# Reading the spill count during the last scatter, and splitting two tiles of the final norm between GpSimd and ScalarE

## Chip, cores and metric

The kernel runs on one core of a Trainium2 chip. The metric is device time in microseconds (us), the median of several executions. The five engines are TensorE (PE in the profile), VectorE (DVE), ScalarE (ACT), GpSimd (POOL) and SyncE (SP, which only issues DMAs here). The core has 16 DMA engines.

## What is computed

One layer of a decoder on 1024 prompt tokens and 64 sample tokens of width 1024: a mixing block, cross attention, a mixture of 32 SwiGLU experts (each token goes to 2), and a last RMSNorm. The change touches the end of the mixture and the last norm:

```python
def rmsnorm(x, g):
    xf = x.astype(jnp.float32)
    y = xf * lax.rsqrt(jnp.mean(xf * xf, axis=-1, keepdims=True) + EPS)
    return (y * g.astype(jnp.float32)).astype(x.dtype)
...
x = x + hier_moe(rmsnorm(x, g_ffn), w_rg, b_rg, w_re, b_re, w_e1, w_e3, w_e2)
...
y_prompt = rmsnorm(xp, g_final)
y_sample = rmsnorm(xs, g_final)
```

## The kernel before

The 1088 tokens lie in nine tiles of 128 rows (tile 8, the sample tokens, has 64), in X, a view of the SBUF region regX. The program of each engine is written out by hand, and semaphores order them.

**Experts.** The sums so far are stored to `token_sums` in HBM. Then for each of 32 experts GpSimd gathers up to 128 token rows by an indirect DMA (`rows_in`), TensorE computes with weights that SyncE streams into a ring (which lies over regX, so X is gone by then), and GpSimd adds the weighted result to `token_sums` by an indirect DMA that accumulates (`rows_out`, L2471).

**Spills.** An expert with over 128 tokens leaves a rest, which a loop of up to 16 steps would handle. VectorE works out the number of such steps between experts 16 and 26 (`spill_counts` to `spill_columns`) and leaves it in `spx[0:1, 16:17]`. Each engine loads this number into a register after `o_go` and skips the loop where it is 0, as with these inputs. In the kernel before it is GpSimd that gives `o_go`, after the waits for the last scatters (`m_sc`), and it loads its own copy after that (L2515); then it signals `s_moe`.

**Final norm.** SyncE waits for `s_moe` and reads the nine tiles of `token_sums` back into X (L989, a helper's line; `sums_back(eng, t)` waits for tile t). ScalarE squares and sums each tile in turn (L1611) and takes a root for each group of tiles (L1614); the groups are `NORMS = [(0, 2), (2, 3), (5, 3), (8, 1)]`, first tile and count. VectorE's `finish(g)` turns the roots of a group into factors by five short steps (L2382, L1632 to L1635) and then multiplies each tile by its factor and by the gain `gfin` (a view of regA) in place (L2386), each product signalling `s_fo`. SyncE stores tile t when `s_fo` is at t + 1 (L1199), in the order 0 to 8. The gain is loaded once TensorE has used the last weights.

Of the kernel before, what the change touches and what calls it, by code (L numbers as in the profile page):

```python
# [33 lines left out]
ALU = mybir.AluOpType  # L34
# [48 lines left out]
def trunk_step(nc, i_, o_):  # L83
    ctx = ExitStack()
    with ctx:
# [3 lines left out]
        def sem(name):  # L89
            return ctx.enter_context(nc.semaphore(name))  # L90
# [205 lines left out]
        junk = regS[:, 4 * D:5 * D]  # L296
        gfin = regA[:, 7168:8192]
        NORMS = [(0, 2), (2, 3), (5, 3), (8, 1)]

        table = nc.dram_tensor("place_table", [P * NPLACE, 2], I32, kind="Internal").ap()  # L300
        xn_dram = nc.dram_tensor("normed_tokens", [N, D], F32, kind="Internal").ap()
# [119 lines left out]
        s_gos = sem("s_gos")  # L421
        s_gate = sem("s_gate")
        s_gtd = sem("s_gtd")
        s_last = sem("s_last")
        m_w = [sem(f"m_w{s}") for s in range(RAW // 2)]
        m_g = [sem("m_g0"), sem("m_g1")]
        m_sc = [sem("m_sc0"), sem("m_sc1")]
# [559 lines left out]
        def _(sp):  # L987
# [204 lines left out]
            sp.wait_ge(s_moe, 1)  # L1192
            for t in range(NT):
                load(X[0:rows_of(t), t], sum_dram[P * t:P * t + rows_of(t), :], m_w[t])
            for t in range(NT):
                sp.wait_ge(s_fo, t + 1)
                dst = o_["y_prompt"][0, P * t:P * t + P, :] if t < NPT else \
                    o_["y_sample"].rearrange("b s d -> (b s) d")
                sp.dma_start(dst, X[0:rows_of(t), t]).then_inc(s_fst, 16)  # L1199
            sp.wait_ge(s_fst, 16 * NT)  # L1200


# [1 line left out]
        def _(act):  # L1204
# [291 lines left out]
            for t in range(NT):  # L1496
                r = rows_of(t)
                emptied(act, ("O2", t, 1))
                if t >= 2:
                    act.wait_ge(s_xnd[t % 2], 16 * (t // 2))  # L1500
                if t < NT - 1:
                    norm_act(3, t, X[:, t, :])
                else:
                    c = 120 + t
                    nc.scalar.activation(junk8[0:r, :], X[0:r, t, :], ACT.Square,
                                         accum_out=stat[0:r, c:c + 1]).then_inc(s_sq[3], 1)
                if t >= 3:
                    filled(act, ("R", t - 3))
                ps, sg = filled(act, ("T", 3, t, 1))
                copy(YT3[t % 3][:, 4:8, 0:r], ps[:, :].rearrange("p (k n) -> p k n", k=4)[:, :, 0:r], sg)  # L1510
                if t == NT - 1:
                    act.wait_ge(s_sq[3], NT)
                    nc.scalar.activation(stat[0:r, c + 10:c + 11], stat[0:r, c:c + 1], ACT.Sqrt,
                                         scale=1.0 / D, bias=small[0:r, 0:1]).then_inc(s_rt[3], 1)
                    act.wait_ge(s_last, 1)
                    nc.scalar.activation(xn2[0:r, t % 2], xn2[0:r, t % 2], ACT.Copy,
                                         scale=stat[0:r, c + 20:c + 21]).then_inc(s_xn[3], 1)

# [86 lines left out]
            for t0, n in NORMS:  # L1605
                for t in range(t0, t0 + n):
                    r = rows_of(t)
                    sums_back(act, t)
                    if t > 0:
                        act.wait_ge(s_fsq, t)  # L1610
                    nc.scalar.activation(junk[0:r, :], X[0:r, t, :], ACT.Square,  # L1611
                                         accum_out=stat[0:r, t:t + 1]).then_inc(s_fsq, 1)
                act.wait_ge(s_fsq, t0 + n)
                nc.scalar.activation(stat[0:r, 10 + t0:10 + t0 + n], stat[0:r, t0:t0 + n], ACT.Sqrt,  # L1614
                                     scale=1.0 / D, bias=small[0:r, 0:1]).then_inc(s_frt, 1)


        @block.vector
        def _(dve):
# [570 lines left out]
                    place(t // GT - 1)  # L2190
            add_bias(NT - 2)
            rstd(3, NT - 1)
            nc.vector.sem_inc(s_last, 1)
            add_bias(NT - 1)
            route(2)
            place(2)
# [139 lines left out]
            for e in range(NE):  # L2336
# [25 lines left out]
                    spill_before()  # L2362
                if e == 26:
                    spill_columns()
            dve.wait_ge(o_go, 1)
            n_spill = dve.value_load(spx[0:1, 16:17], min_val=0, max_val=SPILL)
            with dve.If(n_spill > 0):
                with dve.Fori(0, SPILL) as q:
# [8 lines left out]
            def finish(g):  # L2377
                t0, n = NORMS[g]
                r = rows_of(t0)
                dve.wait_ge(s_frt, g + 1)  # L2380
                a, root, r0, tmp, out = (stat[0:r, c + t0:c + t0 + n] for c in (280, 10, 300, 310, 20))
                link(ts_(a, stat[0:r, t0:t0 + n], 1.0 / D, EPS, ALU.mult, ALU.add))  # L2382
                inv_root(a, root, r0, tmp, out)
                for j in range(n):
                    x = X[0:r, t0 + j, :]
                    stt(x, x, out[:, j:j + 1], gfin[0:r, :], ALU.mult, ALU.mult).then_inc(s_fo, 1)  # L2386

            dve.wait_ge(s_cst, 32)
            for g in range(len(NORMS)):
# [4 lines left out]
        def _(g):  # L2394
# [104 lines left out]
            for e in range(NE):  # L2499
# [4 lines left out]
                if 12 <= e < 12 + NT:  # L2504
                    g.wait_ge(s_plc, (e - 12) // GT + 1)
                    for c in range(2):
                        place_rows(e - 12, c)
            rows_out(NE - 1)
            for s in range(2):
                g.wait_ge(m_sc[s], 16 * (NE // 2))  # L2510
            g.wait_ge(s_scat, 16 * 2 * NT)
            g.wait_ge(s_gtd, 16)

            g.sem_inc(o_go, 1)
            n_spill = g.value_load(spx[0:1, 16:17], min_val=0, max_val=SPILL)  # L2515
            with g.If(n_spill > 0):  # L2516
                with g.Fori(0, SPILL) as q:
                    g.wait_ge(o_ix, 16 * q + 16)
# [6 lines left out]
                    scatter(0, oix, o_sc)  # L2525
                g.wait_ge(o_sc, 16 * (SPILL + 1))
            g.sem_inc(s_moe, 1)  # L2527
            g.wait_ge(s_outs, 16 * 6)
            g.wait_ge(s_kout, 32)

# [97 lines left out]
```

## Time and profile before

| | us |
|---|---|
| median of 3 executions (1067.07 to 1067.89) | 1067.43 |
| the profiled execution | 1065.81 |
| its span | 1064.0 |
| PE / DVE / ACT / POOL busy | 999.0 / 638.3 / 541.6 / 197.6 |
| bytes moved by the DMA engines | 203.06 MB |

Times in the rows further down are us from the start of the span. An engine with a q (POOLq, SPq) is its sequencer, which issues DMAs, loads registers and branches. A line number is that of kernel.py. "Landing" is the time at which a DMA's completion is signalled, counted from its issue. A row with x3 holds three instructions that follow each other.

### The profile page before, as it was taken

How to read it: one execution, taken by the hardware profiler on the slowest of the kernel's cores; microseconds unless marked ns; L12 is line 12 of the kernel's file. 1: busy time of each engine (PE TensorE's matmuls, PEld its weight loads, DVE VectorE, ACT ScalarE, POOL GpSimd, SP SyncE). 2: the span in 40 equal slices, each digit the busy share in tenths (PEclk: the TensorE clock that was granted, in tenths of full speed). 3: DMA queues.
4: the chain of work that ended last, by engine and by line, in shares of the span. 5: the costliest groups of instructions: out<-in, count | busy, mean ns of one | idle time of the engine just before them, and what ended most of it. 6: DMA issues, size and time to landing. Idle time of an engine off the chain costs nothing. (4 is left out here: it accounts for less than half of the span.)

```text
span 1064.0 us, 14237 instructions
## 1 busy us (share of the span) xinstructions
PE 999.0 (94%) x5327; PEld 848.1 (80%) x5327; DVE 638.3 (60%) x1175; ACT 541.6 (51%) x918; POOL 197.6 (19%) x136
## 2 busy tenths in 40 slices
PE   8999999999999999999999999948999999999970
PEld 6998999798887689999655878847888888888850
DVE  4526756345654650002664125677999999999935
ACT  6644333305221532213545012255999999999944
POOL 0003211100000021200000300011333375642220
PEclk9999999999999999999999999967999999999995
DMA  9701111244000653103563005487999999999738
GB/s 314 217 1 59 57 42 40 99 139 173 1 1 0 225 177 113 40 20 127 232 256 139 1 37 201 159 310 300 396 392 391 384 364 390 382 387 393 284 55 335
DMA packets 55211, 203.06 MB, mean 191 GB/s; under 512 B 10710, under 2 KB 19423, under 8 KB 41575
## 3 DMA queue, kind: packets, MB, share of 16 engines
q1 hardware_dynamic: 44327, 181.61, 44.9%
q0 software_dynamic: 10816, 20.54, 7.6%
q8 instruction: 43, 0.70, 0.3%
q14 instruction: 25, 0.20, 0.1%
HBM read 185.06 MB, written 32.83 MB: 205 GB/s over the span
## 5 line engine op out<-in xcount | busy, mean ns | idle before, releaser
L527 PE MATMUL bank<-regA_r,regW_r 128*128 128x352 f32 (+1 forms) x456 | 148.8, 326 | 0.0
L526 PE MATMUL bank<-regA_r,regW_r 128*128 128x352 f32 (+1 forms) x456 | 148.7, 326 | 0.0
L359 POOL TENSOR_TENSOR regW_r<-regW,regW_r 128x1024 fp32r<-128x1024 f32 x19 | 47.1, 2477 | 348.7 <-ACT regW_r L346 348.6
L1525 ACT ACTIVATE regY_r<-expert_w 128x1024 fp32r<-128x1024 f32 x105 | 108.9, 1062 | 1.0 <-PE bank L527 0.9
L525 PE MATMUL bank<-expert_w_r,regS_r 128*128 128x512 f32 x256 | 103.4, 404 | 0.0
L1525 ACT ACTIVATE regW_r<-expert_w 128x1024 fp32r<-128x1024 f32 x87 | 90.2, 1061 | 6.7 <-PE bank L527 6.7
L2292 DVE TENSOR_TENSOR expert_w_r<-expert_w,regY_r 128x1024 fp32r<-128x1024 f32 x74 | 89.0, 1218 | 0.0
L525 PE MATMUL bank<-regY_r,regW_r 128*128 128x352 f32 (+1 forms) x264 | 87.3, 331 | 0.5 <-ACT regB L1206 0.5
L526 PEld LDWEIGHTS bank<-regA_r,regW_r 128*128 128x128 f32 x456 | 85.9, 188 | 0.4
L527 PEld LDWEIGHTS bank<-regA_r,regW_r 128*128 128x128 f32 x456 | 85.6, 188 | 0.0
L2466 POOL DMA_INDIRECT regW<-normed_tokens,idx x32 | 44.0, 1374 | 200.0 <-DVE idx L2201 119.6
L1215 ACT ACTIVATE regS<-regX 128x1024 f32<-128x1024 f32 (+1 forms) x17 | 18.0, 1060 | 119.9 <-DVE regX L1877 119.9
L527 PE MATMUL bank<-regW_r,regA_r 128*128 128x384 f32 (+3 forms) x216 | 76.4, 354 | 0.0
L2471 POOL DMA_INDIRECT token_sums<-regS,idx x32 | 55.5, 1735 | 106.2 <-ACT regS L1548 102.6
L1877 DVE TENSOR_TENSOR regX<-regX,bank 128x512 f32<-128x512 f32 (+1 forms) x36 | 24.1, 686 | 77.8 <-PE bank L527 77.7
L527 PE MATMUL bank<-regY_r,regS_r 128*128 128x512 f32 x180 | 70.4, 391 | 0.0
L526 PE MATMUL bank<-regY_r,regB_r 128*128 128x512 f32 (+1 forms) x176 | 68.6, 390 | 0.0
L1952 DVE TENSOR_REDUCE stat<-bank 128x2 f32<-128x512 f32 x16 | 11.0, 690 | 93.9 <-PE bank L699 93.9
L2292 DVE TENSOR_TENSOR expert_w_r<-expert_w,regW_r 128x1024 fp32r<-128x1024 f32 x54 | 64.8, 1217 | 0.0
L527 PE MATMUL bank<-regY_r,regA_r 128*128 128x512 f32 (+1 forms) x164 | 64.0, 390 | 0.0
L525 PE MATMUL bank<-regB_r,regW_r 128*128 128x352 f32 (+1 forms) x192 | 63.0, 328 | 0.0
L526 PE MATMUL bank<-regY_r,regS_r 128*128 128x512 f32 x148 | 57.7, 390 | 0.0
(363 smaller groups left out, 2408.1 us busy)
## 6 DMA issues: line engine op xcount, KB each, us to landing
expert_w<-in_we SPq DMA_DIRECT2D x96, 1024.0 KB, 13.3
regY<-in_cache_mem_v SPq DMA_DIRECT2D x6, 1024.0 KB, 7.2
regW<-in_wbc SPq DMA_DIRECT2D x11, 512.0 KB, 3.6
regS<-in_x_prompt SPq DMA_DIRECT2D x8, 512.0 KB, 6.5
regX<-in_x_prompt SPq DMA_DIRECT2D x8, 512.0 KB, 6.6
regW<-in_wq SPq DMA_DIRECT2D x8, 512.0 KB, 3.6
regA<-in_kct SPq DMA_DIRECT2D x4, 1024.0 KB, 7.9
token_sums<-regX SPq DMA_DIRECT2D x8, 512.0 KB, 2.9
```

The lines of the kernel that those rows point to most:

```text
L359: eng.tensor_tensor(lo, raw, hi.bitcast(F32), ALU.subtract).then_inc(w_lo[name], 1)
L525: nc.tensor.matmul(out, stays[0], moves[1], start=first, stop=False)
L526: nc.tensor.matmul(out, stays[1], moves[0], start=False, stop=False)
L527: ins = nc.tensor.matmul(out, stays[0], moves[0], start=False, stop=last)
L1215: nc.scalar.activation(dst[0:r, :], src[0:r], ACT.Square, accum_out=stat[0:r, c:c + 1]).then_inc(s_sq[s], 1)
L1525: nc.scalar.activation(part_hi[u % HI], part_raw[n % RAW], ACT.Copy).then_inc(m_wh, 1)
L1877: tt(x, x, ps[0:r, :], ALU.add).then_inc(sg, 1)
L1952: link(nc.vector.tensor_reduce(stat[:, 276:278], ps[:, :].rearrange("p (a m) -> p a m", a=2), axis=AX.X, op=ALU.max, negate=True))
L2292: tt(part_lo[n % RAW], part_raw[n % RAW], part_hi[u % HI].bitcast(F32), ALU.subtract).then_inc(m_ul, 1)
L2466: g.indirect_dma_start(out=XG[s], out_offset=None, in_=xn_dram, in_offset=bass.IndirectOffsetOnAxis(ap=ix[:, 0:1], axis=0), bounds_check=l ...
L2471: g.indirect_dma_start(out=sum_dram, out_offset=bass.IndirectOffsetOnAxis(ap=ix[:, 0:1], axis=0), in_=YO[s], in_offset=None, bounds_check= ...
```

## The change

It has two parts. The spill count: VectorE gives `o_go` itself, behind the last step of the count (expert 26), and GpSimd loads the count before it waits for the last scatters. The final norm: for tiles 6 and 7 GpSimd multiplies X by the gain into another place (`WEIGHTED`, in regY, where weights lay), and ScalarE scales that by the tile's factor, once tile 5's product on VectorE has signalled. VectorE leaves these two tiles out. SyncE keeps its order of stores and takes tiles 6 and 7 from the new place. `s_last`, which ordered a step much earlier, is renamed and shared with GpSimd's products.

```diff
+        POOL_ROWS = (6, 7)
+        WEIGHTED = [regY[:, 3072 + D * j:4096 + D * j] for j in range(len(POOL_ROWS))]
...
-            for t in range(NT):
-                sp.wait_ge(s_fo, t + 1)
+            by_dve, by_pool = [t for t in range(NT) if t not in POOL_ROWS], list(POOL_ROWS)
+            for t in (0, 1, 2, 3, 4, 5, 6, 7, 8):
+                if t in by_pool:
+                    sp.wait_ge(s_fo_act, by_pool.index(t) + 1)
+                else:
+                    sp.wait_ge(s_fo, by_dve.index(t) + 1)
...
-                sp.dma_start(dst, X[0:rows_of(t), t]).then_inc(s_fst, 16)
+                sp.dma_start(dst, WEIGHTED[by_pool.index(t)] if t in by_pool else X[0:rows_of(t), t]).then_inc(s_fst, 16)
...
+            for j, t in enumerate(POOL_ROWS):
+                act.wait_ge(s_rooted_weighted, 1 + j + 1)
+                act.wait_ge(s_fo, NORMS[2][0] + 1)
+                nc.scalar.activation(WEIGHTED[j], WEIGHTED[j], ACT.Copy, scale=stat[:, 20 + t:21 + t]).then_inc(s_fo_act, 1)
...
                 if e == 26:
                     spill_columns()
-            dve.wait_ge(o_go, 1)
+                    nc.vector.sem_inc(o_go, 1)
             n_spill = dve.value_load(spx[0:1, 16:17], min_val=0, max_val=SPILL)
...
-                for j in range(n):
-                    x = X[0:r, t0 + j, :]
-                    stt(x, x, out[:, j:j + 1], gfin[0:r, :], ALU.mult, ALU.mult).then_inc(s_fo, 1)
+                for t in range(t0, t0 + n):
+                    if t not in POOL_ROWS:
+                        x = X[0:r, t, :]
+                        stt(x, x, stat[0:r, 20 + t:21 + t], gfin[0:r, :], ALU.mult, ALU.mult).then_inc(s_fo, 1)
...
             rows_out(NE - 1)
+            g.wait_ge(s_scat, 16 * 2 * NT)
+            g.wait_ge(s_gtd, 16)
+            g.wait_ge(o_go, 1)
+            n_spill = g.value_load(spx[0:1, 16:17], min_val=0, max_val=SPILL)
             for s in range(2):
                 g.wait_ge(m_sc[s], 16 * (NE // 2))
-            g.wait_ge(s_scat, 16 * 2 * NT)
-            g.wait_ge(s_gtd, 16)
-
-            g.sem_inc(o_go, 1)
-            n_spill = g.value_load(spx[0:1, 16:17], min_val=0, max_val=SPILL)
...
             g.sem_inc(s_moe, 1)
+            g.wait_ge(s_cst, 32)
+            for j, t in enumerate(POOL_ROWS):
+                sums_back(g, t)
+                g.tensor_tensor(WEIGHTED[j], X[:, t, :], gfin[:, :], ALU.mult).then_inc(s_rooted_weighted, 1)
```

GpSimd's instructions after the scatters (rows of a scatter, the load of the count, the branch around the loop), in the kernel before:

```order
L2471 DMA token_sums<-regS,idx 1088x1024 [waits m_yo1,m_yo0] x6
L2515 TENSOR_LOAD spx [waits s_gtd,s_scat,m_sc0,m_sc1]
L2515 ISA x2
L2516 COMPARE_AND_BRANCH
L2517 UNCONDITIONAL_BRANCH
L2517 ISA
```

and in the changed one:

```order
L2483 DMA token_sums<-regS,idx 1088x1024 [waits m_yo1,m_yo0] x6
L2524 TENSOR_LOAD spx [waits o_go,s_gtd,s_scat]
L2524 ISA x2
L2527 COMPARE_AND_BRANCH [waits m_sc1,m_sc0]
L2528 UNCONDITIONAL_BRANCH
L2528 ISA
```

The load no longer waits for the last scatters (`m_sc0`, `m_sc1`), and the branch does.

The end of GpSimd's program, before (the end of the spill loop, and the end of the block):

```order
L2523 ISA
L2471 DMA token_sums<-regS,oix 1088x1024 [waits o_yo,s_waited]
L2517 REGISTER_ALU
L2517 COMPARE_AND_BRANCH
L2516 UNCONDITIONAL_BRANCH [waits o_sc]
L85 UNCONDITIONAL_BRANCH [waits s_kout,s_outs]
```

and now:

```order
L2534 ISA
L2483 DMA token_sums<-regS,oix 1088x1024 [waits o_yo,s_waited]
L2528 REGISTER_ALU
L2528 COMPARE_AND_BRANCH
L2527 UNCONDITIONAL_BRANCH [waits o_sc]
L2542 TENSOR_TENSOR regY<-regX,regA 128x1024 [waits m_w6,s_cst]
L2542 TENSOR_TENSOR regY<-regX,regA 128x1024 [waits m_w7]
L85 UNCONDITIONAL_BRANCH [waits s_kout,s_outs]
```

Two products of 128x1024 stand behind the signal of the sums, each waiting for its tile's read (`m_w6`, `m_w7`).

VectorE's last two groups of the norm, tiles 5 to 7 and tile 8, before:

```order
L1632 RECIPROCAL stat<-stat 128x3 [waits s_dv]
L1633 SCALAR_TENSOR_TENSOR stat<-stat 128x3 [waits s_dv]
L1634 TENSOR_TENSOR stat<-stat 128x3 [waits s_dv]
L1635 SCALAR_TENSOR_TENSOR stat<-stat 128x3 [waits s_dv]
L2386 SCALAR_TENSOR_TENSOR regX<-regX,stat,regA 128x1024 [waits s_dv]
L2386 SCALAR_TENSOR_TENSOR regX<-regX,stat,regA 128x1024 x2
L2382 TENSOR_SCALAR stat<-stat 64x1 [waits s_frt]
L1632 RECIPROCAL stat<-stat 64x1 [waits s_dv]
L1633 SCALAR_TENSOR_TENSOR stat<-stat 64x1 [waits s_dv]
L1634 TENSOR_TENSOR stat<-stat 64x1 [waits s_dv]
L1635 SCALAR_TENSOR_TENSOR stat<-stat 64x1 [waits s_dv]
L2386 SCALAR_TENSOR_TENSOR regX<-regX,stat,regA 64x1024 [waits s_dv]
```

and now:

```order
L1643 RECIPROCAL stat<-stat 128x3 [waits s_dv]
L1644 SCALAR_TENSOR_TENSOR stat<-stat 128x3 [waits s_dv]
L1645 TENSOR_TENSOR stat<-stat 128x3 [waits s_dv]
L1646 SCALAR_TENSOR_TENSOR stat<-stat 128x3 [waits s_dv]
L2398 SCALAR_TENSOR_TENSOR regX<-regX,stat,regA 128x1024 [waits s_dv]
L2393 TENSOR_SCALAR stat<-stat 64x1 [waits s_frt]
L1643 RECIPROCAL stat<-stat 64x1 [waits s_dv]
L1644 SCALAR_TENSOR_TENSOR stat<-stat 64x1 [waits s_dv]
L1645 TENSOR_TENSOR stat<-stat 64x1 [waits s_dv]
L1646 SCALAR_TENSOR_TENSOR stat<-stat 64x1 [waits s_dv]
L2398 SCALAR_TENSOR_TENSOR regX<-regX,stat,regA 64x1024 [waits s_dv]
```

Of the products of 128x1024 in the third group one is left, tile 5's, and the steps for tile 8 follow it directly.

## Rows read from the trace of the kernel before

**Rows 1.** Busy us by stretch and engine, granted clock, DMA share, GB/s.
```profile
1037.50:1039.50 2.00, 0.00 (x0) 0.00 (x0) 0.00 (x0) 0.75 (x1) 0.00 (x0) 0.50 0.00 0
...
1052.50:1062.00 9.50, 0.00 (x0) 0.00 (x0) 7.87 (x16) 2.35 (x6) 0.00 (x0) 0.50 1.03 420
```

**Rows 2.** The chain that ended last: start us, us, what.
```profile
1037.88 0.51 POOLq L2515
...
1038.70 0.06 POOLq L2516
...
1038.93 0.34 SPq L989
...
1040.73 7.05 DMA regX<-token_sums
```

**Rows 3.** Timeline of DVE, final norm: start us, us, engine line op, count.
```profile
1050.33 3.68 DVE L2386 SCALAR_TENSOR_TENSOR regX<-regX,stat,regA 128x1024 f32<-128x1024 f32 x3
...
1054.92 3.68 DVE L2386 SCALAR_TENSOR_TENSOR regX<-regX,stat,regA 128x1024 f32<-128x1024 f32 x3
...
1059.44 1.28 DVE L2386 SCALAR_TENSOR_TENSOR regX<-regX,stat,regA 64x1024 f32<-64x1024 f32 x1
```

**Rows 4.** SyncE, stores of tiles 5, 7, 8, each with us to landing.
```profile
1056.23 0.33 SPq L1199 DMA_DIRECT2D out_y_prompt<-regX  x1
...
out_y_prompt<-regX SPq DMA_DIRECT2D x1, 512.0 KB, 4.1
...
1058.63 0.33 SPq L1199 DMA_DIRECT2D out_y_prompt<-regX  x1
...
out_y_prompt<-regX SPq DMA_DIRECT2D x1, 512.0 KB, 4.2
...
1060.74 0.49 SPq L1199 DMA_DIRECT2D out_y_sample<-regX  x1
...
out_y_sample<-regX SPq DMA_DIRECT2D x1, 256.0 KB, 2.9
```

**Rows 5.** DMA issues from 540 to 740 us: KB each, median us to landing.
```profile
token_sums<-regX SPq DMA_DIRECT2D x8, 512.0 KB, 2.9
```

**Rows 6.** Instructions of line 359: ns min/median/max, first and last start.
```profile
L359 POOL TENSOR_TENSOR regW_r<-regW,regW_r x19: 2360/2410/3249, 57.2 to 461.5; 128x1024 fp32r<-128x1024 f32 x19
```

**Rows 7.** Timeline of ACT, squares of tiles 6 and 7.
```profile
1050.42 1.06 ACT L1611 ACTIVATE regS<-regX 128x1024 f32<-128x1024 f32 x1
...
1052.07 1.06 ACT L1611 ACTIVATE regS<-regX 128x1024 f32<-128x1024 f32 x1 [0.50 <-DMA regX<-token_sums]
```

**Rows 8.** POOL and DVE where they overlap; two lines' ns min/median/max.
```profile
129.37 2.40 POOL L359 TENSOR_TENSOR regW_r<-regW,regW_r 128x1024 fp32r<-128x1024 f32 x1 [14.86 <-ACT regW_r L346]
...
130.57 2.28 DVE L1746 TENSOR_TENSOR regS<-regS,regW 128x1024 f32<-128x1024 f32 x1 [5.96 <-ACT regS L1314]
...
L1746 DVE TENSOR_TENSOR regS<-regS,regW x6: 1224/1225/2279, 130.6 to 218.8; 128x1024 f32<-128x1024 f32 x6
...
159.43 2.80 POOL L359 TENSOR_TENSOR regW_r<-regW,regW_r 128x1024 fp32r<-128x1024 f32 x1 [9.61 <-ACT regW_r L346]
...
159.88 2.49 DVE L1822 TENSOR_TENSOR regS<-regS 128x128 f32<-128x128 f32 x1
...
L1822 DVE TENSOR_TENSOR regS<-regS x6: 222/329/2492, 119.4 to 163.6; 128x176 f32<-128x176 f32 x2, 64x160 f32<-64x160 f32 x1, 128x160 f32<-128x160 f32 x1, 128x128 f32<-128x128 f32 x1
...
373.36 5.84 POOL L359 TENSOR_TENSOR regW_r<-regW,regW_r 128x1024 fp32r<-128x1024 f32 x2 [120.21 <-ACT regW_r L346]
...
374.95 1.98 DVE L1894 TENSOR_TENSOR regY_r<-regY,regY_r 128x1024 fp32r<-128x1024 f32 x1 [1.37 <-ACT regY_r L1390]
```

**Rows 9.** Timeline of ACT, three conversions in a row.
```profile
1002.83 3.03 ACT L1525 ACTIVATE regW_r<-expert_w 128x1024 fp32r<-128x1024 f32 x3
```

**Rows 10.** SyncE's waits: us in total, times, longest.
```profile
SPq L989 <- POOLq L2527: 0.2, 1, 0.2
```

More of the change, by code:

```diff
@@ L423, in trunk_step @@
         s_gtd = sem("s_gtd")
-        s_last = sem("s_last")
+        s_fo_act = sem("s_fo_act")
+        s_rooted_weighted = sem("s_rooted_weighted")
         m_w = [sem(f"m_w{s}") for s in range(RAW // 2)]
@@ L1514, in _ @@
                                          scale=1.0 / D, bias=small[0:r, 0:1]).then_inc(s_rt[3], 1)
-                    act.wait_ge(s_last, 1)
+                    act.wait_ge(s_rooted_weighted, 1)
                     nc.scalar.activation(xn2[0:r, t % 2], xn2[0:r, t % 2], ACT.Copy,
@@ L2192, in _ @@
             rstd(3, NT - 1)
-            nc.vector.sem_inc(s_last, 1)
+            nc.vector.sem_inc(s_rooted_weighted, 1)
             add_bias(NT - 1)
```

## The prediction

> **What bounds the kernel now.** The change touches only the end of the program, so I read the end. The stretches come first [rows 1]: from 1052.5 to 1062 us the 16 DMA engines are full (share 1.03) and move 420 GB/s, with DVE busy for 7.87 us of 9.5 beside them; from 1037.5 to 1039.5 us nothing moves at all. The chain that ended last [rows 2] fills this gap: the last scatter lands at 1037.88, GpSimd loads the spill count (0.51 us for the load alone), branches at 1038.70, and only then does SyncE issue the first read of the sums, at 1038.93. The fifth of these reads takes 7.05 us, since it queues behind four others.
>
> Then the final norm. DVE's timeline [rows 3] shows products in packs: three in 3.68 us, of 1.28 us each, so one begins each 1.20 us. Tile 5's is the first of the pack at 1054.92 and ends at 1056.20; tiles 6 and 7 follow, then four short steps, then tile 8, which ends at 1060.72. Each product is stored as it ends [rows 4]: tile 5 issued at 1056.23 and landed 4.1 us later (1060.33), tile 7 at 1058.63 with 4.2 us (1062.83), tile 8 at 1060.74 with 2.9 us (1063.64). A store of 512 KB with a quiet queue takes 2.9 us too [rows 5]. So the 4.1 and 4.2 us are queueing: the landings of tiles 5 and 7 lie 2.50 us apart, 1.25 each, and tile 8 with half the bytes comes 0.8 us after tile 7. **The end is held by two things at once**: DVE hands over a tile each 1.20 us, and the DMA engines write one each 1.25 us. Taking work from DVE alone could give only the last 0.2 us or so (1062.83 + 0.63 for half a tile, against 1063.64).
>
> **The change, part by part.**
>
> 1. The count is read while the scatter flies. GpSimd's steps from 1037.88 to 1038.70 leave the path [rows 2]: -0.82 us. SyncE, ScalarE, VectorE and TensorE read theirs earlier too, as DVE now signals at expert 26; SyncE's issue of the reads waits for nothing else. ScalarE's table load (1.28 us) comes earlier as well, beside the scatter: no gain, since ScalarE waits for the first read anyway. Bounds: 0 (something else holds SyncE) to -1.05 (all of the gap between landing and issue). I take -0.82.
>
> 2. DVE loses the products of tiles 6 and 7: 2 x 1.20 = -2.40 us before tile 8's product, nothing before tile 5's.
>
> 3. GpSimd gains two products of 128x1024 with both inputs in SBUF. No row has this pair, but the same form of subtraction took 2.41 us in the median on GpSimd [rows 6]. Tile 6 lands by 1050.42 and tile 7 at 1052.07, where ScalarE begins on them [rows 7]; 0.82 earlier that is 1049.6 and 1051.2, in the middle of DVE's products of tiles 2 to 4. So the question is what the two engines do to each other.
>
> The places where both run answer it [rows 8]. At 129.37 GpSimd starts its subtraction (ends 131.77); DVE starts a TENSOR_TENSOR with two SBUF inputs at 130.57 and ends at 132.85, 2.28 us where this line's median is 1.225: it did nothing until GpSimd was through and then took 1.08. A whole block thus costs 2.40 - (1.225 - 1.08) = 2.25 us. At 159.88 a DVE op of 128x128 took 2.49 where its line's median is 0.33, a block of 2.16; GpSimd's, issued at 159.43 under a running DVE op, took 2.80, so it had waited too. At 374.95 (1.98) and in the 5.84 of two GpSimd ops they take turns. All of these pairs read only SBUF on both engines. The product of the norm reads X and the gain, both in SBUF. I take 2.2 us for each, 4.4 together; bounds 0 (they overlap freely) and 2.4 each.
>
> Those rows are TENSOR_TENSOR, and the norm's product is SCALAR_TENSOR_TENSOR, which no row shows beside GpSimd. Here the Trainium skill, "SBUF — State Buffer", section "Who interferes with whom", says that any DVE instruction with two SBUF inputs and a GpSimd instruction that reads SBUF exclude each other for a whole instruction. By it the sum would be the one below. Without the page, the case that only TENSOR_TENSOR collides stays open; its sum is that of the first rival.
>
> DVE is late as a consequence: tile 5's product ends at 1056.20 - 0.82 + 4.4 = 1059.8. GpSimd takes turns and is through by some 1056.6, so it is never the one waited for. Tile 8's product ends at 1060.72 - 0.82 - 2.4 + 4.4 = 1061.9.
>
> 4. ScalarE gains two scalings, and they wait for tile 5's product (s_fo at 6), though all that they need of DVE is ready before it. Nothing is queued behind them on ScalarE, but SyncE stores in the order 0 to 8, so tile 8 waits behind both. An ACTIVATE of 128x1024 takes 1.06 [rows 7] and three in a row 3.03 [rows 9], so the two end 1.1 and 2.1 us after tile 5's: tile 6 is issued at 1060.9, tile 7 at 1061.9, tile 8 0.4 later (0.33 us of issue), at 1062.3, against 1060.74 before. All 6 other stores go as before.
>
> 5. Landing. The queue was idle before tile 5 by now: 1059.8 + 2.9 = 1062.7. Tile 6 lands at 1062.7 + 1.25 = 1063.95 (its own 1060.9 + 2.9 is 1063.8), tile 7 at 1065.2, tile 8 at 1065.2 + 0.8 = 1066.0. Before: 1063.64. **Sum +2.3 us.** The bounds: if the four stores don't queue, tile 8 lands at 1062.3 + 2.9 = 1065.2, +1.6; blocks of 2.4 give +2.7; blocks of 2.0 give +1.9.
>
> The Trainium skill, "DMA: Bandwidth & Descriptors", section "Where 436 GB/s comes from", has about 358 GB/s as the HBM side's limit per core. The trace has 420 GB/s in just this stretch, so the measurement decides; by the page a tile would cost 1.46 us instead of 1.25, and the end would come some 0.5 us later still.
>
> The profiled execution took 1065.81 us (span 1064.0), 1.6 less than the median of 1067.43; the change adds the same to both, so 1067.43 + 2.3 = **1069.7 us**. A measurement of this kernel can tell about 0.2%, 2.1 us, from no change, so the forecast lies just beyond that line.
>
> **Rivals.**
> - **No collision.** If the product of the norm isn't held up by GpSimd, DVE ends tile 5 at 1055.4, ScalarE has tile 7 by 1057.5, and the DMA engines are the only bound: landings at 1.25 each from a start 0.82 earlier, tile 8 at 1062.83 - 0.82 + 0.63 = 1062.6, -1.0 us: 1066.4. It is not slower at all. It decides as soon as the two blocks together cost under 1.2 us or so: tile 5 would land at 1055.4 + 2.9 = 1058.3 by itself, and the queue gets to it at 1060.33 - 0.82 = 1059.5 only. For it: no row has this DVE form beside GpSimd. Against it: every pair with two SBUF inputs in [rows 8] collided. 0.10.
> - **Half of it.** One of the two products falls where DVE is idle or in its short steps and costs nothing. Then tile 5 is issued at 1057.6 and lands at 1060.5, and tiles 6 to 8 follow at 1061.75, 1063.0 and 1063.8: +0.1, 1067.5. For it: before the pack of tile 2 and between the packs DVE has four or five short steps and a wait. Against it: tile 6 lands (1050.4) just after that pack begins (1050.33), and a short step with two SBUF inputs is blocked as well. 0.12.
> - **The early count brings nothing**, because the chain of GpSimd after the scatter hides another wait of the same length (SyncE waits only 0.2 us for GpSimd in the table of waits [rows 10], and the landing of the scatter itself isn't in a row of its own). Then part 1 is 0: +3.1, 1070.5. 0.08.
> - **GpSimd late**: its first product in a long time is slow, or it has to let several DVE ops pass, so that tile 6 or 7 isn't there when tile 5's product ends. From 3 us later than I put it this decides; with 4 us it gives 1071. Against it: its two ops at 373 came after 120 us of idling and took 5.84 together, turns with DVE included [rows 8]. 0.04.
>
> **Numbers.** The forecast has 0.66, within 1068.8 to 1070.4 (bounds of blocks, of the queue, and 0.3 us of spread between runs). Of it a bit over half lies beyond 2.1 us, 0.36, and 0.30 within. Slower: 0.36 + 0.08 + 0.04 = 0.48. Within 0.2%: 0.30 + 0.12 + 0.08 = 0.50. Faster by over 2.1 us: 0.02, since even without any collision the DMA engines allow 1.0. The range leaves out the first rival and the top of the last: 1067.2 to 1070.9.
>
> **What would show it.** In the changed profile: the first read of the sums is issued about 0.25 us after the last scatter's landing, not 1.05. Two DVE products of the tiles 2 to 4 take some 3.4 us instead of 1.28, each beside a GpSimd product of 2.4 to 3.6 us. ScalarE's two scalings begin at tile 5's product's end. The stores of tiles 5 to 8 land 3 us after issue, and the DMA share drops below 0.8 between 1054 and 1060, where it was 1.03. Wrong would be: DVE products all at 1.28 (the first rival), a first read that comes no earlier (the third), or a ScalarE that waits for GpSimd (the fourth).

## The result

The changed kernel takes 1070.8 us (median of 20 executions, 1067.32 to 1072.79), the kernel before 1068.34 us (20 executions, 1065.69 to 1070.47). The medians lie 2.5 us apart. The ratio formed from all executions is 1.0019 with a 95% interval from 1.0011 to 1.0026: slower by 2.0 us (1.2 to 2.8). The interval does not include 1, but the size is just about what the prediction took for the least that can be told (2.1 us). The profiled execution took 1071.62 us.

Its span is 1069.8 us against 1064.0, which is more than the change did. GpSimd's first scatter starts at 751.74 us here and at 748.53 in the kernel before, and its 29th at 1015.02 and 1011.81: the 263.28 us between them are the same to the hundredth, and the 3.21 us of offset were there before the experts began; their cause is open. So I count from a mark next to the change, the issue of the last scatter. From there to the end of the span it is 1064.0 - 1033.82 = 30.18 us before and 1069.8 - 1037.05 = 32.75 us now: **+2.57 us**.

**The start of the tail.** The chain that ended last in the changed kernel, start us, us, what:

```profile
1037.05 4.12 DMA token_sums<-regS,idx
...
1041.26 0.06 POOLq L2527
...
1041.48 0.34 SPq L992
...
1043.29 7.14 DMA regX<-token_sums
```

The last scatter is issued at 1037.05 and lands 4.12 us later (before: 1033.82 to 1037.88, 4.06). Then comes the branch, and the first read of the sums is issued at 1041.48, 0.31 us after the landing, where [rows 2] had 1.05: 0.74 us gained. The fifth read takes 7.14 us, as before.

**The collision.** Timelines of DVE and POOL in the changed kernel, final norm:

```profile
1052.96 1.28 DVE L2398 SCALAR_TENSOR_TENSOR regX<-regX,stat,regA 128x1024 f32<-128x1024 f32 x1
...
1054.17 3.36 DVE L2398 SCALAR_TENSOR_TENSOR regX<-regX,stat,regA 128x1024 f32<-128x1024 f32 x1
...
1057.45 3.37 DVE L2398 SCALAR_TENSOR_TENSOR regX<-regX,stat,regA 128x1024 f32<-128x1024 f32 x1
...
1053.07 3.38 POOL L2542 TENSOR_TENSOR regY<-regX,regA 128x1024 f32<-128x1024 f32 x1 [14.47 <-DMA regX<-token_sums]
...
1056.43 3.31 POOL L2542 TENSOR_TENSOR regY<-regX,regA 128x1024 f32<-128x1024 f32 x1
...
1052.96 7.85 DVE L2398 SCALAR_TENSOR_TENSOR regX<-regX,stat,regA 128x1024 f32<-128x1024 f32 x3
...
1061.73 1.28 DVE L2398 SCALAR_TENSOR_TENSOR regX<-regX,stat,regA 128x1024 f32<-128x1024 f32 x1
...
1063.85 1.28 DVE L2398 SCALAR_TENSOR_TENSOR regX<-regX,stat,regA 64x1024 f32<-64x1024 f32 x1
```

The first two rows and the third are tiles 2, 3 and 4. Tile 2's product began 0.11 us before GpSimd's and took its usual 1.28; GpSimd's took 3.38, since it first waited for that one. Tile 3's took 3.36, tile 4's 3.37: each stood until GpSimd was through. The pack of three takes 7.85 us where [rows 3] had 3.68, 4.17 more for two products of GpSimd, 2.09 each. Tile 5's product ends at 1063.01, 4.26 us later after the first read's issue than before (21.53 against 17.27).

**The scalings and the stores.** ACT's two scalings, and SyncE's last stores, each with its time to landing:

```profile
1063.11 2.19 ACT L1626 ACTIVATE regY<-regY,stat 128x1024 f32<-128x1024 f32 x2 [3.89 <-DVE regX L2398]
...
1063.05 0.33 SPq L1206 DMA_DIRECT2D out_y_prompt<-regX  x1
...
out_y_prompt<-regX SPq DMA_DIRECT2D x1, 512.0 KB, 2.6
...
1064.29 0.33 SPq L1206 DMA_DIRECT2D out_y_prompt<-regY  x1
...
out_y_prompt<-regY SPq DMA_DIRECT2D x1, 512.0 KB, 2.7
...
1065.70 0.49 SPq L1206 DMA_DIRECT2D out_y_sample<-regX  x1
...
out_y_sample<-regX SPq DMA_DIRECT2D x1, 256.0 KB, 3.7
```

ScalarE begins when tile 5's product is there. Tile 5's store has nothing ahead of it and lands after 2.6 us, where [rows 4] had 4.1; tiles 6 and 7 take 2.7 and 3.0 us, each landing 1.3 us behind the tile before. Tile 8's takes 3.7, since it is issued 0.4 us after tile 7's. Tile 8 lands at 1069.4.

**The DMA engines** by stretch (the columns of [rows 1]: DMA share and GB/s last):

```profile
1057.00:1059.50 2.50, 0.00 (x0) 0.00 (x0) 2.50 (x2) 2.16 (x6) 2.50 (x1) 0.50 1.03 419
1060.00:1061.50 1.50, 0.00 (x0) 0.00 (x0) 1.40 (x5) 0.00 (x0) 0.00 (x0) 0.50 0.16 63
1063.00:1064.00 1.00, 0.00 (x0) 0.00 (x0) 0.83 (x7) 0.89 (x1) 0.00 (x0) 0.50 0.15 57
```

They were full to the end before [rows 1] and now run dry twice, at 1060 and at 1063, because DVE hands over no tile. From 1064 on they are full again to the end.

### The profile page after: what moved, and what is told of

Read it like the earlier page. It is cut to its first block, busy times and chain, and to the rows that moved or that the text cites. A ratio compares the mean times of both kernels' runs of the same rounds, so it can differ in the third digit from the quotient of the medians.

```text
span 1069.8 us, 14242 instructions
## 1 busy us (share of the span) xinstructions
PE 1000.1 (93%) x5327; PEld 849.2 (79%) x5327; DVE 640.1 (60%) x1173; ACT 543.9 (51%) x920; POOL 204.5 (19%) x138
## 4 chain that ended last, share of the span: by engine, by line
PE 59%; DVE 17%; DMA 2%; ACT 2%; issue 2%; ACTq 0%; SPq 0%; POOLq 0%; DVEq 0%
PE bank L528 15%; PE bank L530 15%; PE bank L529 15%; DVE expert_w_r L2303 6%; PE bank L496 4%; DVE expert_w_r L2309 3%; PE bank L702 3%; PE bank L505 2%; PE bank L893 1%; DVE regS_r L2321 1%; DVE regX L2398 1%; PE bank L773 1%; PE bank L753 1%; DMA regW<-normed_tokens,idx 1%; DMA regX<-token_sums 1%
## 5 line engine op out<-in xcount | busy, mean ns | idle before, releaser
L1222 ACT ACTIVATE regS<-regX 128x1024 f32<-128x1024 f32 (+1 forms) x17 | 18.0, 1059 | 120.0 <-DVE regX L1888 120.0
```

## The experiments

Times of the tail come from one trace each; ratios to the kernel before with their intervals from several runs of both. "Tail" is counted from the issue of the last scatter, "from the first read" from the issue of the first read of the sums, "from the first landing" from the start of the first square on ScalarE, and "from the pack" from the start of VectorE's products of tiles 2 to 4, where the first collision comes. The first three carry the spread of the DMA engines: the scatter lands after 3.7 to 4.1 us in these traces and the first read after 3.3 to 4.0, and the pack starts between 7.6 and 8.6 us after the first square. The last leaves that out, and it repeats to 0.1 us between traces of the same norm.

| kernel | ratio (95% interval) | tail | from the first read | from the first landing | from the pack |
|---|---|---|---|---|---|
| before | 1 | 30.18 | 25.07 | 21.37 | 13.67 |
| changed | 1.0019 (1.0011 to 1.0026) | 32.75 | 28.32 | 25.00 | 16.84 |
| changed again (e12) | 1.0012 (0.9999 to 1.0025) | 32.72 | 28.75 | 24.79 | 16.79 |
| count alone (e1) | 0.9990 (0.9978 to 1.0002) | 29.22 | 25.16 | 21.30 | 13.69 |
| count alone again (e11) | 0.9993 (0.9979 to 1.0008) | 29.03 | 25.01 | 21.24 | 13.62 |
| norm alone (e2) | 1.0022 (1.0011 to 1.0033) | 33.30 | 28.21 | 24.49 | 16.87 |
| gain in PSUM (e3) | 0.9990 (0.9980 to 1.0000) | 30.11 | 26.02 | 22.41 | 13.77 |
| halves in SBUF (e4) | 1.0017 (1.0005 to 1.0028) | 32.77 | 28.68 | 24.96 | 17.35 |
| idle products (e5) | 1.0028 (1.0018 to 1.0037) | 33.72 | 29.36 | 25.43 | 17.82 |
| one tile (e6) | 1.0006 (0.9995 to 1.0017) | 30.73 | 26.39 | 22.35 | 14.75 |
| scalings early (e7) | 1.0022 (1.0011 to 1.0032) | 32.28 | 28.30 | 24.53 | 16.92 |
| gain in PSUM, scalings early (e8) | 0.9992 (0.9981 to 1.0003) | 29.71 | 25.60 | 21.61 | 14.00 |
| stores held (e9) | 1.0008 (0.9997 to 1.0020) | 31.28 | 27.08 | 23.66 | 15.95 |
| product in idle time (e10) | 0.9987 (0.9973 to 1.0002) | 31.23 | 26.93 | 23.16 | 14.80 |

My theory: the early count gives 0.75 us, and GpSimd's products stop VectorE's for 2.1 us each, since both engines read two SBUF tensors. The rivals: the two parts depend on each other; the products are slow for another reason (the stores and reads that pass through the same tiles, ScalarE's wait, the order of the stores).

### The parts apart

e1 has only the count's part (the edit against the kernel before, with `o_go` given behind `spill_columns`); e2 is the changed kernel with this edit undone:

```diff
-            dve.wait_ge(o_go, 1)
+                    nc.vector.sem_inc(o_go, 1)
...
+            g.wait_ge(o_go, 1)
+            n_spill = g.value_load(spx[0:1, 16:17], min_val=0, max_val=SPILL)
             for s in range(2):
                 g.wait_ge(m_sc[s], 16 * (NE // 2))
-            g.sem_inc(o_go, 1)
-            n_spill = g.value_load(spx[0:1, 16:17], min_val=0, max_val=SPILL)
```

> Only the early load of the count; the norm as before. The tail is counted from the issue of the last scatter to the end of the span: 30.2 us in the kernel before, 32.8 in the changed one. Theory (the two parts are independent, the count gives 0.75 us, the collision of GpSimd and VectorE takes it back and more): tail 29.4 to 29.6, landing of the scatter to first read 0.3 us, nine products of 1.28 us, total 0.7 us below the kernel before. Rival (the early count brings nothing to the end, since the DMA engines or a later wait bound it): first read earlier but tail 30.0 to 30.2.

> Only the split of tiles 6 and 7; the count as before. Theory: tail 33.4 to 33.6 (32.8 + 0.75), two products of VectorE of 3.3 to 3.4 us beside GpSimd's two of 3.3, total 2.7 to 3.3 us above the kernel before. Rival (the two parts interact, for instance the late landing of tile 7's read, 14.9 us after the first read's issue against 13.1, comes from the early count): tile 7 lands after 13.1 us here and the tail is 32 or less.

The count alone has a tail of 29.22 us, 0.96 less than before (0.74 of it between landing and first read, 0.3 a scatter that landed after 3.75 us), and from the first read on it is the kernel before (25.16 against 25.07). The norm alone takes 33.30 us, 3.12 more than before, all of it behind the first read. Both tails lie just under the ranges I gave (29.4 to 29.6, and 33.4 to 33.6). -0.96 and +3.12 give +2.16 against the +2.57 of both together; the 0.4 us left are no more than what the landings of the scatter and of the first read differ by. Without these landings the sum closes: from the pack the count alone is the kernel before (13.62 and 13.69 against 13.67), and the norm alone is the changed kernel (16.87 against 16.84 and 16.79). Tile 7's square starts 13.0 us after the first read's issue in e2, as its rival had it, but the tail is 33.30 and not 32. So the parts add up, and neither rival stands.

### Is it the second SBUF input?

ScalarE has nothing to do between the scatter and the first read. In e3 it copies the gain into two free PSUM banks there, and VectorE takes it from them in halves of 512 columns; VectorE waits for these two copies before its first product, and SyncE's count of ScalarE's signals allows for them. All the rest, GpSimd's products included, is the changed kernel, which the edit is against. e4 is the control, with the loop over halves and `gfin[0:r, 512 * h:512 * h + 512]` in place of the bank.

```diff
+            act.wait_ge(s_cst, 32)
+            for h in range(2):
+                nc.scalar.activation(bank[B_TX[h]][:, :], gfin[:, 512 * h:512 * h + 512], ACT.Copy).then_inc(s_fo_act, 1)
...
-                        x = X[0:r, t, :]
-                        stt(x, x, stat[0:r, 20 + t:21 + t], gfin[0:r, :], ALU.mult, ALU.mult).then_inc(s_fo, 1)
+                        for h in range(2):
+                            x = X[0:r, t, 512 * h:512 * h + 512]
+                            ins = stt(x, x, stat[0:r, 20 + t:21 + t], bank[B_TX[h]][0:r, :], ALU.mult, ALU.mult)
+                        ins.then_inc(s_fo, 1)
```

> The changed kernel, with the gain copied by ScalarE into two PSUM banks while it waits for the first read, and VectorE's products taking it from there in two halves of 512 columns, so that they read SBUF once. GpSimd's products and ScalarE's scalings stay. Theory (two engines that both need a second SBUF read exclude each other): no product of VectorE is stretched (two halves take 1.3 to 1.4 us), GpSimd's two take 2.4 each, tile 5's product ends 4 us earlier, and the DMA engines bound the end: tail 29.2 to 29.8. Rival (the products are slow for another reason, such as the stores and reads that move through X at the same time): the same stretches of 3.3 us, tail 32.8 or more.

> The control for the one with the gain in PSUM: the products of VectorE in the same two halves, but both inputs in SBUF. Theory: GpSimd waits for one half and not for a whole product, VectorE loses the same 2.1 us or so per product of GpSimd: tail 32.6 to 33.4. Rival (the halves themselves let the engines interleave): tail below 31.

Timelines of DVE and POOL with the gain in PSUM:

```profile
1051.93 4.04 DVE L2402 SCALAR_TENSOR_TENSOR regX<-regX,stat,bank 128x512 f32<-128x512 f32 x6
1055.88 0.85 DVE L2396 TENSOR_SCALAR stat<-stat 128x3 f32<-128x3 f32 x1
1056.77 0.17 DVE L1646 RECIPROCAL stat<-stat 128x3 f32<-128x3 f32 x1
...
1052.03 4.67 POOL L2547 TENSOR_TENSOR regY<-regX,regA 128x1024 f32<-128x1024 f32 x2 [14.89 <-DMA regX<-token_sums]
```

Beside GpSimd's two products, which take 4.67 us together, VectorE's six halves take 4.04 us, 1.35 per tile: none of them waits. The control:

```profile
1051.65 8.25 DVE L2399 SCALAR_TENSOR_TENSOR regX<-regX,stat,regA 128x512 f32<-128x512 f32 x6
...
1051.79 5.57 POOL L2544 TENSOR_TENSOR regY<-regX,regA 128x1024 f32<-128x1024 f32 x2 [14.01 <-DMA regX<-token_sums]
```

8.25 us for the same six halves (GpSimd waits for a half only, hence 5.57 for its two). The products differ in nothing but where the gain lies, and with it in PSUM the 4.2 us are gone. That settles the cause of the stretch: the product's second input in SBUF. The time follows: 0.9990 against 1.0017. The tail of e3 is 30.11 us, though, and I had put it at 29.2 to 29.8. The reads of the second group came late in this execution: the pack starts 12.25 us after the first read's issue (before: 11.40), and from the pack to the end it is 13.77 us against 13.67. Tile 5's product ends 2.2 us earlier after the first read than in the changed kernel (19.3 against 21.5), not the 4 us expected, for the same reason and because of the row that follows.

One row of e3 I had not expected: VectorE's TENSOR_SCALAR on 3 columns of `stat` took 0.85 us instead of 0.17. It reads one SBUF tensor; it began at 1055.88 and ended at 1056.73, just behind GpSimd's second product (1056.70). In e8 the same step takes 0.89 us and ends just behind GpSimd too (1056.55 against 1056.51). So that form is held up as well, [rows 8] have none of it, and "two inputs in SBUF" is not the whole rule.

### The collision by itself

e5 is the count alone with all nine products on VectorE, and GpSimd's two products beside them, whose result nobody uses. VectorE waits before tiles 6 and 7 until GpSimd has read them.

```diff
+            for j, t in enumerate(POOL_ROWS):
+                sums_back(g, t)
+                g.tensor_tensor(WEIGHTED[j], X[:, t, :], gfin[:, :], ALU.mult).then_inc(s_idle, 1)
...
+                    if t0 + j in POOL_ROWS:
+                        dve.wait_ge(s_idle, POOL_ROWS.index(t0 + j) + 1)
```

> The early count, and the norm as before with all nine products on VectorE, but GpSimd computes its two products of tiles 6 and 7 as well and nobody uses them (VectorE multiplies these two tiles only once GpSimd has read them). This measures the collision by itself. Counted from the issue of the first read of the sums to the end of the span: 25.1 us before, 25.2 with the count alone, 28.3 in the changed kernel. Theory: 2.1 us lost per product of GpSimd and nothing taken from VectorE: 25.1 + 4.2 = 29.3, two products stretched to 3.3 us. Rival (part of the loss in the changed kernel is ScalarE's scalings and the order of the stores, and a product of GpSimd alone costs VectorE less): below 28.3.

Timelines of DVE and POOL with the idle products:

```profile
1051.68 7.86 DVE L2391 SCALAR_TENSOR_TENSOR regX<-regX,stat,regA 128x1024 f32<-128x1024 f32 x3
...
1060.45 3.68 DVE L2391 SCALAR_TENSOR_TENSOR regX<-regX,stat,regA 128x1024 f32<-128x1024 f32 x3
...
1051.82 6.63 POOL L2535 TENSOR_TENSOR regY<-regX,regA 128x1024 f32<-128x1024 f32 x2 [14.49 <-DMA regX<-token_sums]
```

7.86 us again in place of 3.68, then an undisturbed pack of 3.68. From the first read it is 29.36 us, 4.2 more than the count alone; 29.3 was expected. From the pack to the end it is 17.82 us, where the changed kernel has 16.84. So taking the two products off VectorE gave back 1.0 us of the 2.4 that VectorE itself was relieved of.

e6 is the changed kernel with only tile 7 split off.

```diff
-        POOL_ROWS = (6, 7)
+        POOL_ROWS = (7,)
```

> The changed kernel with only tile 7 split off. Counted from the first read's issue: theory 25.9 to 26.2 (one block of 2.1 us, one product of 1.2 us less before tile 8's product: 25.1 + 0.9), total some 0.2 us from the kernel before. Rival (the loss comes from waiting for ScalarE after tile 5 and not from the number of blocks): near the 28.3 of two tiles.

One block: the pack of three takes 5.77 us, 2.09 more than 3.68. From the first read it is 26.39 us, a little over the range I gave (25.9 to 26.2), with a first landing 4.0 us after the issue that was late by 0.3; the rival's 28.3 is far. The stretch of the pack goes by the number of blocks. The end does not quite: from the pack it is 1.1 us later with one block (14.75 against 13.67) and 3.2 with two. An explanation that no run tests by itself: before the change tile 5's store stood in the DMA queue (4.1 us to landing against 2.6 in e6), which hides part of the first block and nothing of the second.

### Where ScalarE's wait matters

In e7 ScalarE waits for the factors of tiles 5 to 7 and not for tile 5's product; e8 does the same with the gain in PSUM. The edit, against the changed kernel:

```diff
-                act.wait_ge(s_rooted_weighted, 1 + j + 1)
-                act.wait_ge(s_fo, NORMS[2][0] + 1)
+                act.wait_ge(s_rooted_weighted, 1 + 2 + 1)
...
+                if g == 2:
+                    nc.vector.sem_inc(s_rooted_weighted, 1)
```

> The changed kernel, but ScalarE waits for the factors of tiles 5 to 7 and not for tile 5's product. Counted from the first read's issue: theory (the end hangs on ScalarE's scalings only by their start behind tile 5's product; then on VectorE's product of tile 8): the scalings begin 1.3 us earlier, tile 8 is issued at 23.7 and the end is at 26.9 to 27.3. Rival (the DMA engines hold the end already): 28.0 or more.

> The gain in PSUM for VectorE, and ScalarE waiting for the factors only. Counted from the first read's issue: with the gain in PSUM alone it was 26.0, where ScalarE's scalings ended at 21.6. Theory: now they end by 20.1, tile 8's product at 21.5, and the end is that of the DMA engines, 24.7 to 25.1; total 1.0 to 1.5 us below the kernel before. It can't go lower, since nine reads and nine stores of 1.25 us each (tile 8 less) with 3.5 us ahead of the first landing make 25. Rival (VectorE's or SyncE's issue of the stores is the bound): 24.2 or less, or still 26.

e7 was a miss. The scalings begin 20.2 us after the first read instead of 21.6, and the end stays at 28.30. SyncE's stores in e7, with their times to landing (the last row holds two, tiles 6 and 7):

```profile
1061.58 0.33 SPq L1206 DMA_DIRECT2D out_y_prompt<-regX  x1
...
out_y_prompt<-regX SPq DMA_DIRECT2D x1, 512.0 KB, 2.6
...
1061.95 1.26 SPq L1206 DMA_DIRECT2D out_y_prompt<-regY  x2
...
out_y_prompt<-regY SPq DMA_DIRECT2D x2, 512.0 KB, 4.1
```

Tile 5 is issued when its product is there and lands after 2.6 us; tiles 6 and 7 follow at once and take 4.1 us (their median), since they stand in the DMA queue. From tile 5's store on, three and a half tiles have to go through, and they take as long whether ScalarE is early or not: 6.3 us from its issue to tile 8's landing in e7, 6.35 in the changed kernel. That is the rival that I had written down for e7, that the DMA engines hold the end already. My first reading of the changed kernel's trace, that ScalarE's wait was the last link, was wrong: that wait lies beside the DMA time. What holds the end is the moment at which tile 5's store is issued, as part 5 of the prediction had it.

With the gain in PSUM (e8) the scalings end by 19.5, and it takes 21.61 us from the first landing against 21.24 to 21.37 of the count alone and the kernel before. The 25.60 from the first read miss my range of 24.7 to 25.1, mostly by what the first landing was late (4.0 us). From the pack it is 14.00 us, 0.3 more than the count alone: between 1059 and 1060 us the DMA share is 0.63, since tile 5's product comes late by the held-up TENSOR_SCALAR (0.89 instead of 0.17 us) and the slower halves (4.04 instead of 3.68 for the pack). So e8 is no faster than the count alone. But it is not the split at no cost: these two delays are its own. That the split could win nothing even without them is argued from the rates before the change, and not shown.

### Two experiments on the DMA engines

e9 has the count alone and issues no store before tile 8's read has landed. In e10, with the count alone too, GpSimd weights tile 0 in the time in which VectorE waits for the first root, and VectorE only scales it; SyncE stores tile 0 from the new place. The edit of e9, then that of e10:

```diff
+            sums_back(sp, NT - 1)
             for t in range(NT):
                 sp.wait_ge(s_fo, t + 1)
```

```diff
+            sums_back(g, 0)
+            g.tensor_tensor(WEIGHTED, X[:, 0, :], gfin[:, :], ALU.mult).then_inc(s_idle, 1)
...
+                    if t0 + j == 0:
+                        dve.wait_ge(s_idle, 1)
+                        ts_(WEIGHTED, WEIGHTED, out[:, 0:1], None, ALU.mult).then_inc(s_fo, 1)
+                        continue
```

> The count alone, and SyncE issues no store before tile 8's read has landed. In the traces so far the DMA rate falls from 420 to about 250 GB/s for 2 us or so, where the first two stores join the last reads. Counted from the start of the first square (the first landing): the end comes 21.3 us after it with the count alone. Theory (reads and stores mixed cost rate, some 0.8 us): tile 8's read lands 0.7 to 1.2 us sooner than 11.05 us after the first, but the stores start up to 1.5 us late, end 21.3 to 22.5. Rival (tile 8's read with its 64 rows is slow by itself): it lands no sooner, end 22.5 or more.

> The count alone, and one product on GpSimd, that of tile 0, which lands while VectorE still waits for the first root; VectorE then scales tile 0 by a TENSOR_SCALAR with one SBUF tensor as input, and does the other eight products as before. Theory (only overlap costs): GpSimd takes 2.4 us, no VectorE product is stretched, VectorE's scaling takes 0.6 to 0.8 us instead of 1.28; the end is still the DMA engines', 21.2 to 21.5 us after the first square's start. Rival (a product on GpSimd costs wherever it stands): some 2 us more, or a stretched operation.

In the kernel before, the rate drops while the first stores join the last reads; in e9 it stays up for longer. Stretches of half a microsecond, first of the kernel before, then of e9:

```profile
1050.50:1051.00 0.50, 0.00 (x0) 0.00 (x0) 0.50 (x1) 0.50 (x1) 0.00 (x0) 0.50 0.90 246
1051.00:1051.50 0.50, 0.00 (x0) 0.00 (x0) 0.50 (x1) 0.50 (x2) 0.00 (x0) 0.50 0.90 270
```

```profile
1051.50:1052.00 0.50, 0.00 (x0) 0.00 (x0) 0.40 (x4) 0.45 (x2) 0.00 (x0) 0.50 1.03 418
1052.00:1052.50 0.50, 0.00 (x0) 0.00 (x0) 0.50 (x1) 0.46 (x1) 0.00 (x0) 0.50 1.06 426
1052.50:1053.00 0.50, 0.00 (x0) 0.00 (x0) 0.50 (x1) 0.50 (x2) 0.00 (x0) 0.50 1.12 336
1053.00:1053.50 0.50, 0.00 (x0) 0.00 (x0) 0.50 (x2) 0.18 (x2) 0.00 (x0) 0.50 0.61 123
...
1054.50:1055.00 0.50, 0.00 (x0) 0.00 (x0) 0.50 (x1) 0.47 (x4) 0.00 (x0) 0.50 0.00 0
```

246 and 270 GB/s against 418 and 426. But e9 drops as well, to 336 and 123 GB/s, as its last read goes through, tile 8's with 64 rows. The rival, that this read is slow by itself, thus holds for part of the drop; how much is the mixing's is not shown. A store of 64 rows is slow too: in e5 tile 8's store moves alone, and its 256 KB keep the DMA engines at a share of 0.80 over 1.5 us, where the 512 KB of tile 5 keep them at 0.86 over as long:

```profile
1060.25:1061.75 1.50, 0.00 (x0) 0.00 (x0) 1.46 (x3) 0.00 (x0) 0.00 (x0) 0.50 0.86 350
...
1067.25:1068.75 1.50, 0.00 (x0) 0.00 (x0) 0.00 (x0) 0.00 (x0) 0.00 (x0) 0.50 0.80 175
```

Half the bytes cost nearly the same time. Nor did the reads land clearly sooner in e9: tile 8's had landed by 10.5 us after the first one (the first store's issue), but tile 7's square begins 9.35 us after the first, against 9.27 in e11 and 9.66 in e1. The DMA engines then stand still for 2 us, until the held stores start, and the end comes 23.66 us after the first landing, later than the 22.5 I allowed. Holding the stores loses more than it can gain.

In e10 nothing collides; timelines of POOL and DVE:

```profile
1041.46 2.35 POOL L2535 TENSOR_TENSOR regY<-regX,regA 128x1024 f32<-128x1024 f32 x1 [6.64 <-DMA regX<-token_sums]
...
1045.17 0.75 DVE L2390 TENSOR_SCALAR regY<-regY,stat 128x1024 f32<-128x1024 f32 x1
1045.83 1.28 DVE L2392 SCALAR_TENSOR_TENSOR regX<-regX,stat,regA 128x1024 f32<-128x1024 f32 x1
```

2.35, 0.75 and 1.28 us: a product on GpSimd costs VectorE nothing where VectorE has no work. Its end came 23.16 us after the first landing, not 21.2 to 21.5, because reads landed late in this execution: VectorE's pack of tiles 2 to 4 starts 0.7 us later after the first landing than before, and it waits 1.1 us more for tile 7, whose square starts 15.4 us after the first read's issue (13.0 to 13.5 in most traces). Without that last wait the 14.80 us from the pack are the 13.7 of the count alone. Over ten executions it is at 0.9987, no different from the count alone.

### The changed kernel and the count again

Both are the same programs as before, run on one chip.

> The count alone once more, for its time: the first measurement was 0.999 of the kernel before with an interval from 0.9978 to 1.0002. From the traces 0.7 to 1.0 us less between the last scatter's issue and the end: 0.9990 to 0.9994. Rival (no gain): 1.0 or above.

> The changed kernel itself once more, beside the count alone on the same chip. Expected: 1.002 of the kernel before, the last scatter's issue to the end 32.6 to 32.9 us, VectorE's two products of 3.3 to 3.4 us again. The time of tile 7's read tells whether its late landing in the first trace (14.9 us after the first read's issue; 13.0 to 13.5 in the other traces) belongs to the change: 14.9 again if so, 13.0 to 13.5 if it was one execution's.

e11 has 0.9993 and a tail of 29.03, e12 1.0012 and 32.72. The pack takes 7.85 us again in e12. Tile 7's square started 14.1 us after the first read's issue, between the two answers that I had set; with 14.9 in the first trace of the changed kernel, 13.0 in e2 and e7, which have the same products, and 15.4 in e10, which has no collision, the late landing comes and goes between traces and needs no part of the change. None of the intervals of the count alone excludes 1 by itself; the gain of 0.74 us is shown by the traces (in e1, e11 and both traces of the changed kernel the first read is issued 0.31 or 0.32 us after the scatter's landing), and not by the times.

## Why the prediction came out as it did

The forecast was +2.3 us, 1069.7 from a median of 1067.43. The ratio gives +2.0 (1.2 to 2.8) and the traces +2.57. The measured 1070.8 us lie 1.1 above the forecast, above its inner range of 1068.8 to 1070.4; 0.9 of it is the kernel before, which had a median of 1068.34 beside it. Step by step:

1. **The count**, -0.82: it is -0.74 (1.05 to 0.31 us). Right. The third rival, that it brings nothing, falls with e1 and e11: from the scatter's landing to the end it is 25.47 and 25.32 us, against 26.12 before.
2. **Two products less before tile 8's**, -2.40: right, the packs and single products keep their 1.20 and 1.28 us. (Five short steps stand before tile 8's product and not four; the times were read rightly.)
3. **The collision**, 2.2 us each: 2.09 each, in five traces (7.85 to 7.86 for two blocks) and in e6 (5.77 for one). The open point, whether the product with three operands collides like the TENSOR_TENSOR of [rows 8], was settled by e3 and e4: it does. The rule of the Trainium skill, "SBUF — State Buffer", section "Who interferes with whom", that I had set beside it agrees with these traces (3.36 and 3.37 us with the gain in SBUF, 4.04 for six halves with it in PSUM). The rivals "no collision" and "half of it" fall. The size was a little high because both engines come off faster after a wait, and the prediction counted only VectorE's share: GpSimd's first product ends 2.21 us after tile 2's (1056.45 and 1054.24), not 2.40, and tile 3's ends 1.08 us after that, not 1.20. 2.21 - 0.12 is the 2.09.
4. **ScalarE's scalings**, ready 1.1 and 2.1 us behind tile 5's product: 1.2 and 2.3, since they start 0.10 us behind it and two in a row take 2.19 and not 2.05. The price of this step is right and its weight was nil: by e7 it hides in the queue.
5. **The landing**: tile 5's store 2.9 us, 2.6 in the trace; the rest 3.3 us behind it, 3.7 in the trace (1065.65 to 1069.4). The two misses cancel, which is luck. Most of the 0.4 us is tile 8: 1.1 us behind tile 7 where the sum had 0.8, and the 0.63 us that the prediction took for half a tile elsewhere is too little as well (e5: half the bytes, nearly the same time). The Trainium skill, "DMA: Bandwidth & Descriptors", section "Where 436 GB/s comes from", has about 358 GB/s on the HBM side, and by it a store would come each 1.46 us (an estimate); in the stretch at 1057 of the changed kernel the rate is 419 GB/s, as the 420 of [rows 1], so the measurement decides again.

Of the signs, the DMA share came only in part: it is 1.03 between 1057 and 1059.5 us, where the prediction had it below 0.8, and 0.16 between 1060 and 1061.5, with a second dip at 1063.

ScalarE never waited for GpSimd, though tile 7's read landed later after the first read's issue than in the kernel before (14.9 us against 13.1); the margin of 3 us in the fourth rival held.

The gain that one might expect of the split, 2.4 us off VectorE, was hardly to be had: before the change the DMA engines wrote one tile each 1.25 us, hard behind VectorE's one each 1.20. With the collision of the products removed (e8) the split ends 0.3 us behind the count alone, counted from the pack, and not ahead of it.

## What to carry to other kernels

Before a tensor operation goes from VectorE to GpSimd, look at what VectorE runs beside it: here each GpSimd product of 2.4 us stopped a VectorE operation with two SBUF inputs for 2.1 us, nearly twice the 1.2 us that it saved. It costs nothing where VectorE is idle (e10) or takes one input from PSUM (e3). And where an engine and the DMA queue behind it go at the same pace, relieving the engine alone can move the end by next to nothing: reading what does not depend on the last transfer while it is in flight was the part that paid.

## What was not expected of the hardware

- A TENSOR_SCALAR of 128x3 on SBUF, one input, waited for GpSimd too (0.85 and 0.89 instead of 0.17 us, e3 and e8), while SCALAR_TENSOR_TENSOR with its tensor inputs in SBUF and PSUM did not (six halves in 4.04 us).
- Where the first stores join the last reads the rate is 246 to 270 GB/s, and reads alone run at 418 to 426 (before, and e9), with the DMA engines' share at 0.9 and over in both. Part of it is the read of the tile with 64 rows, which is slow alone too (336 GB/s at a share of 1.12 in e9); the rest is not separated.
- A store of 256 KB from 64 rows keeps the DMA engines busy nearly as long as one of 512 KB from 128 (0.80 against 0.86 of 1.5 us, e5).
- The first scatter starts between 747.9 and 753.3 us in these traces (748.53 before, 749.12 in e2, 751.74 in the changed kernel, 751.85 in e1, 753.25 in e6, 747.94 in e10), and executions of the kernel before alone range over 5 to 6 us, while the 263.28 us from the first scatter to the 29th are 263.22 to 263.30 in all traces. A change of 2 us at the end is read better from a mark in the trace than from a whole time.
